# RWKV-7 scan of a hybrid diffusion step: a second pair of array quadrants for the products inside a chunk

## The chip, the cores and the metric

The kernel runs on one core of a Trainium2 chip. A core has five engines with an instruction stream each: TensorE (PE; its weight loads are shown apart as PEld), VectorE (DVE), ScalarE (ACT), GpSimd (POOL) and SyncE (SP), which only issues DMAs here. They wait for each other by semaphores. The metric is the device time of one launch in microseconds; the kernel before has a median of 6051.32 us over three runs, 6049.71 to 6054.07.

## What is computed

One inference step of a backbone with two layers. Each layer has attention beside a bidirectional RWKV-7 time mixing, an output projection, and a retrieval over 16384 experts. The change is in the RWKV part. There 8 heads of width 64 carry a 64x64 state through 640 tokens (128 of context and 512 of a latent grid), once in each direction, and the two results are added:

```python
def _rwkv_step(S, inp):
    r, w, kk, a, k, v = inp
    sk = jnp.einsum('bdhvk,bdhk->bdhv', S, kk)
    S = S * w[..., None, :] - sk[..., :, None] * (kk * a)[..., None, :] + v[..., :, None] * k[..., None, :]
    return S, jnp.einsum('bdhvk,bdhk->bdhv', S, r)
...
    xs = (to_scan(shared(r)), to_scan(per_dir(w)), to_scan(shared(kk)),
          to_scan(per_dir(a)), to_scan(per_dir(kmod)), to_scan(shared(v)))
    s_final, y = lax.scan(_rwkv_step, s0.astype(jnp.float32), xs)
    y = jnp.moveaxis(y, 0, 1)
    y = y[:, :, 0] + jnp.flip(y[:, :, 1], axis=1)
```

## The kernel before

`rwkv_scan` does not step through tokens. It goes through 5 tiles of 128 tokens (`TILES`), each of two chunks of 64 (`CHUNK`), for two streams, one for each direction, that run side by side. `rwkv_scan` is called once a layer, so a launch has 10 tiles for each stream. Nothing in it is a loop on the device: the five tiles are written out, and so is every product. (The two layers are a device loop around it.)

Inside a chunk the token-to-token dependence is a triangular system of 64x64 for each head. The kernel inverts it by doubling: `M` is the inverse for blocks of some size, `MT` its transpose, and a *level* makes them one size larger, from `LT` (the strictly triangular matrix) masked to that level: X = (masked L) x M, then M -= MT' x X and MT -= X' x MT. `LEVELS` is 6, and the loop runs lv = 1 to 5; the last has no update of M.

All in fp32. A product is 64x64x64 for one head `j` (8) and one chunk `c` (2), so 16 products for one stream, 32 for both. The array is four quadrants of 64x64: a product takes the rows (partitions) where its operands lie and the columns (partitions) where its result goes. `quads` is the order (0,0), (1,1), (0,1), (1,0) of row half and column half; `pair_product` and `to_channels` use all four. `chunk_product` reads and writes `rows(c)`: it uses the two quadrants on the diagonal. A fp32 product stands in the trace as two matmul records and two weight-load records, a 128x128 transpose as one and one.

The order of the work is written out by hand: each engine has its own list for a tile, in the same order in every tile, and waits on counting semaphores (`x_done`, `x_taken`, `m_ready`, ...).

- TensorE (`block.tensor`): two pair products a stream for L and P (bank 0, 1), two more for M's start and F (banks 2, 3); `to_tokens`, transposes of a, b and k (L1217); k x r (`GT`); q1 (L1258), the first correction; the levels (L1202); za and zq, the inverse applied to a's tokens and to q1; `to_channels` products (L1211); then the state steps (L1312, L1320).
- ScalarE: copies from PSUM to SBUF: `tokens` (L985: a_tok, nb, kt), `take_q1` (L991), `take_x` (L996), `take_zq`, `take_a`; and `decays` (L980), the exponentials of the next tile, after levels 2 and 3.
- VectorE: `masked` (L1080), M + identity (L1114), MT made from LT (L1117) + identity (L1120), `update` (L1089 for M, L1093 for MT), `ab` of the next tile (L1072 to L1076) after levels 3 and 4, the copy of za (L1132), and the sums of outputs and states (L1135 to L1180).
- GpSimd: `level_mask` (L1038), the masked L of each level, two levels ahead of use, and `rk` (L1050), k and r of the next tile.

`st.ps` is a stream's half of PSUM: four banks of 512 columns. `w.ident2` is a 64x64 identity, once in each half of the rows.

Of the kernel before, what the change touches and what calls it, by code (L numbers as in the profile page):

```python
# [20 lines left out]
ALU = mybir.AluOpType  # L21
# [3 lines left out]
P = 128  # L25
# [915 lines left out]
def rwkv_scan(nc, s, w, layer):  # L941
# [4 lines left out]
             "q1_taken", "pt_ready", "x_done", "x_taken", "mx_done", "mtx_done", "m_ready", "mt_ready", "za_done",  # L946
# [4 lines left out]
    with stage(nc, *["r%d_%s" % (d, n) for d in range(2) for n in names]) as (block, *sems):  # L951
# [20 lines left out]
        def _(act):  # L972
# [10 lines left out]
            def tokens(st, i, n, dst, bank, sign):  # L983
                act.wait_ge(st.e["tr_done"], 3 * i + n)
                nc.scalar.activation(dst.rearrange("p (h b) k -> p h b k", h=2),  # L985
                                     st.ps[:, bank, :].rearrange("p (b h k) -> p h b k", h=2, k=CHUNK), ACT.Copy,
                                     scale=sign).then_inc(st.e["tr_taken"], 1)

            def take_q1(st, i):
                act.wait_ge(st.e["q1_done"], i + 1)  # L990
                nc.scalar.activation(st.q1, st.ps[:, 1, :].rearrange("p (j v) -> p j v", v=CHUNK),  # L991
                                     ACT.Copy).then_inc(st.e["q1_taken"], 1)

            def take_x(st, i, lv):
                act.wait_ge(st.e["x_done"], 5 * i + lv)
                nc.scalar.activation(st.X, st.ps[:, 0, :].rearrange("p (j v) -> p j v", v=CHUNK),  # L996
                                     ACT.Copy).then_inc(st.e["x_taken"], 1)

            def take_zq(st, i):
                act.wait_ge(st.e["zq_done"], i + 1)  # L1000
                nc.scalar.activation(st.zq, st.ps[:, 2, :].rearrange("p (j v) -> p j v", v=CHUNK),
                                     ACT.Copy).then_inc(st.e["zq_taken"], 1)

            def take_a(st, i):
                act.wait_ge(st.e["a_done"], i + 1)
                for c in range(2):
                    nc.scalar.activation(st.A[:, c].rearrange("p b k -> p (b k)"), st.ps[:, 3 * c, 0:256],
# [4 lines left out]
            for i in range(TILES):  # L1012
                for n, bank, sign in ((1, 0, 1.0), (2, 1, -1.0), (3, 0, 1.0)):
                    for st in streams:
                        tokens(st, i, n, (st.a_tok, st.nb, st.kt)[n - 1], bank, sign)
                for st in streams:
                    take_q1(st, i)
                for lv in range(1, LEVELS):
# [46 lines left out]
        def _(dve):  # L1065
# [18 lines left out]
            def update(st, i, lv):  # L1084
                e = st.e
                if lv < LEVELS - 1:
                    dve.wait_ge(e["mx_done"], 4 * i + lv)
                    dve.wait_ge(e["m_ready"], 5 * i + lv)
                    v.tensor_tensor(st.M, st.M, st.ps[:, 2, :].rearrange("p (j t) -> p j t", t=CHUNK),  # L1089
                                    ALU.subtract).then_inc(e["m_ready"], 1)  # L1090
                dve.wait_ge(e["mtx_done"], 5 * i + lv)
# [11 lines left out]
            for i in range(TILES):  # L1103
# [11 lines left out]
                marks = []  # L1115
                for st, link in zip(streams, links):
                    marks.append(link.mark(v.tensor_tensor(st.MT, st.LT, st.mask(4), ALU.mult)))  # L1117
                for st, at in zip(streams, marks):
                    dve.wait_ge(st.e["chain"], at)
                    v.tensor_tensor(st.MT, st.MT, st.ident, ALU.add).then_inc(st.e["mt_ready"], 1)  # L1120
                for st in streams:
                    masked(st, i, 3, st.GT, 2, 0, 2)
                for lv in range(1, LEVELS):
                    for st in streams:
                        update(st, i, lv)
                    if lv == 3 and i + 1 < TILES:
                        ab(streams[0], i + 1)
                    if lv == 4 and i + 1 < TILES:
                        ab(streams[1], i + 1)
                for st in streams:  # L1130
                    dve.wait_ge(st.e["za_done"], i + 1)
                    v.tensor_copy(st.za, st.ps[:, 1, :].rearrange("p (j t) -> p j t", t=CHUNK)).then_inc(st.e["za_taken"], 1)  # L1132
                for st in streams:
                    dve.wait_ge(st.e["r_done"], i + 1)
                    v.tensor_tensor(st.rr.rearrange("p b (c t) -> p c b t", c=2),  # L1135
                                    st.ps[:, 1:3, 0:256].rearrange("p c (b t) -> p c b t", b=RB),
                                    st.rT.rearrange("p b (c t) -> p c b t", c=2), ALU.add).then_inc(st.e["r_taken"], 1)
                for st in streams:
# [6 lines left out]
                    v.tensor_tensor(y_of(st, i), st.ps[:, 1:3, 0:256].rearrange("p c (b t) -> p c b t", b=RB),  # L1145
                                    y_of(st, i), ALU.add).then_inc(st.e["y0_taken"], 1)
                for n in range(2):
                    marks = []
                    for st, link in zip(streams, links):
# [9 lines left out]
                        marks.append(link.mark(v.tensor_tensor(st.sum, st.ps[:, 3 * c, 0:256], now, ALU.add)))  # L1159
# [1381 lines left out]
```

## Time and profile before

| | us |
|---|---|
| median of three runs | 6051.32 |
| lowest, highest | 6049.71, 6054.07 |
| the profiled execution, its own time | 6041.68 |
| its span in the trace | 6039.9 |
| first scan, from 519 to 813 | 294 |
| second scan, from 3484 to 3778 | 294 |

| engine, of the whole span | busy us | share |
|---|---|---|
| TensorE, matmul | 5538.2 | 92% |
| TensorE, weight load | 5352.4 | 89% |
| VectorE | 3316.2 | 55% |
| ScalarE | 2205.1 | 37% |
| GpSimd | 2219.7 | 37% |

The experts take most of the span. The two scans are 588 us of 6039.9. A matmul record's length in the trace (218 ns) is that of one product's way through the array, several of them overlap; how fast products follow each other is read from starts, not from lengths. "issue" behind the idle time of an engine means that it waited for nothing that the profile shows. "PEclk" is the granted clock of TensorE as a share of 2.4 GHz.

### The profile page before, as it was taken

To read this page: it belongs to the slowest core of one execution; us is meant where nothing else is said; L and a number is where in the kernel's file an instruction comes from. 1 tells how busy PE (TensorE), PEld (TensorE's weight loads), DVE (VectorE), ACT (ScalarE), POOL (GpSimd) and SP (SyncE) were. 2 spreads that over 40 slices of the span, in tenths; PEclk is the share of its full clock that TensorE was granted. 3 is DMA by queue.
4 is the path that set the end of the run, shared out by engine and by line. 5 is a ranking of instruction groups with operands and counts; after the bars stand their busy time and mean duration, and the time that the engine had idled before them with its cause. 6 is when DMAs were issued, how large, how long until landed. Compare 5 with 4: busy or idle time off the path is not lost. (4 is left out here: it accounts for less than half of the span.)

```text
span 6039.9 us, 130192 instructions
## 1 busy us (share of the span) xinstructions
PE 5538.2 (92%) x53444; PEld 5352.4 (89%) x53444; DVE 3316.2 (55%) x6178; ACT 2205.1 (37%) x2717; POOL 2219.7 (37%) x1048
## 2 busy tenths in 40 slices
PE   5877897899999999999979688799999999999999
PEld 2757887899999999999968488699999999999999
DVE  4545547756565146566645465496555541656655
ACT  4433222355555622222224332224555564222221
POOL 0002222365566543343300032225556564334332
PEclk8988998999999999999989799899999999999999
DMA  5200012245555565445411000224555556554553
GB/s 200 81 34 13 5 59 84 96 164 177 175 176 182 165 220 174 163 165 175 142 71 51 19 7 17 84 69 135 177 174 180 176 168 226 167 170 163 170 167 111
DMA packets 304063, 778.41 MB, mean 129 GB/s; under 512 B 23724, under 2 KB 109228, under 8 KB 299496
## 3 DMA queue, kind: packets, MB, share of 16 engines
q1 hardware_dynamic: 303592, 771.81, 37.9%
q8 instruction: 335, 5.49, 0.4%
q14 instruction: 136, 1.11, 0.1%
HBM read 586.38 MB, written 185.34 MB: 128 GB/s over the span
## 5 line engine op out<-in xcount | busy, mean ns | idle before, releaser
L2135 POOL TENSOR_TENSOR ex_v_lo<-ex_v_raw,ex_v_hi 128x1024 fp32r<-128x1024 f32 x256 | 692.1, 2724 | 1071.4 <-ACT ex_v_hi L2041 1071.4
L335 PE MATMUL ex_ps<-tk_h_hi,tk_u_hi 128*128 128x320 f32 x4096 | 966.4, 317 | 44.0 <-POOL tk_u_lo L2123 34.8
L2123 POOL TENSOR_TENSOR tk_u_lo<-tk_u_raw,tk_u_hi 128x1024 fp32r<-128x1024 f32 x256 | 655.5, 2561 | 883.2 <-ACT tk_u_hi L2011 870.5
L335 PE MATMUL ex_ps<-ex_wa_hi,ex_v_hi 128*128 128x320 f32 x4096 | 935.1, 310 | 18.8 <-issue 18.8
L335 PE MATMUL ex_ps<-tk_h_hi,tk_u_lo 128*128 128x320 f32 x4096 | 938.3, 310 | 3.8 <-issue 3.8
L335 PE MATMUL ex_ps<-tk_h_lo,tk_u_hi 128*128 128x320 f32 x4096 | 937.0, 310 | 0.0
L335 PE MATMUL ex_ps<-ex_wa_hi,ex_v_lo 128*128 128x320 f32 x4096 | 934.8, 309 | 0.0
L335 PE MATMUL ex_ps<-ex_wa_lo,ex_v_hi 128*128 128x320 f32 x4096 | 934.7, 309 | 0.0
L2295 DVE TENSOR_TENSOR ex_y<-ex_y,ex_ps 128x640 f32<-128x640 f32 x496 | 405.9, 818 | 671.4 <-PE ex_ps L335 666.7
L335 PEld LDWEIGHTS ex_ps<-tk_h_hi,tk_u_hi 128*128 128x128 f32 x4096 | 680.0, 190 | 46.1 <-POOL tk_u_lo L2123 35.7
L335 PEld LDWEIGHTS ex_ps<-ex_wa_hi,ex_v_hi 128*128 128x128 f32 x4096 | 686.5, 188 | 19.3 <-issue 19.3
L335 PEld LDWEIGHTS ex_ps<-tk_h_hi,tk_u_lo 128*128 128x128 f32 x4096 | 688.0, 189 | 4.8 <-issue 4.8
L335 PEld LDWEIGHTS ex_ps<-tk_h_lo,tk_u_hi 128*128 128x128 f32 x4096 | 689.5, 189 | 0.0
L335 PEld LDWEIGHTS ex_ps<-ex_wa_lo,ex_v_hi 128*128 128x128 f32 x4096 | 686.2, 188 | 0.0
L335 PEld LDWEIGHTS ex_ps<-ex_wa_hi,ex_v_lo 128*128 128x128 f32 x4096 | 686.1, 188 | 0.0
L2254 DVE CUSTOM_DVE_ANT_0 ex_ps<-x,tk_silu 128x512 f32<-128x512 f32 x384 | 346.2, 901 | 611.9 <-DMA x<-in_w_mod_rows 599.8
L2130 POOL TENSOR_TENSOR x<-tk_one_hot,tk_g_hk 128x512 f32<-128x512 bf16 x320 | 556.6, 1745 | 82.0 <-PE ex_ps L1944 77.8
L2035 ACT ACTIVATE tk_grid<-ex_ps 128x512 f32<-128x512 f32 x320 | 356.3, 1113 | 474.3 <-PE ex_ps L1944 474.3
L2041 ACT ACTIVATE ex_v_hi<-ex_v_raw 128x1024 fp32r<-128x1024 f32 x256 | 268.3, 1048 | 693.9 <-PE ex_ps L335 693.9
L2046 ACT ACTIVATE ex_wa_hi<-x 128x640 fp32r<-128x640 f32 x256 | 189.4, 740 | 619.9 <-DVE x L2280 619.9
L2028 ACT ACTIVATE x<-tk_one_hot 128x512 f32<-128x512 bf16 x320 | 391.3, 1223 | 17.0 <-issue 9.1
L2286 DVE TENSOR_TENSOR ex_wa_lo<-x,ex_wa_hi 128x640 fp32r<-128x640 f32 x256 | 374.1, 1461 | 30.4 <-ACT ex_wa_hi L2046 21.3
(341 smaller groups left out, 8333.9 us busy)
## 6 DMA issues: line engine op xcount, KB each, us to landing
tk_u_raw<-in_expert_u SPq DMA_DIRECT2D x256, 512.0 KB, 4.2
ex_v_raw<-in_expert_v SPq DMA_DIRECT2D x256, 512.0 KB, 3.6
act_spill<-tk_act_e SPq DMA_DIRECT2D x256, 320.0 KB, 2.3
grid_scratch<-tk_grid SPq DMA_DIRECT2D x160, 512.0 KB, 5.4
ex_g<-grid_scratch SPq DMA_DIRECT2D x64, 1280.0 KB, 11.0
x<-in_w_mod_rows SPq DMA_DIRECT2D x192, 256.0 KB, 4.6
ex_a<-act_spill SPq DMA_DIRECT2D x32, 1280.0 KB, 7.8
x<-act_spill SPq DMA_DIRECT2D x32, 1280.0 KB, 8.0
```

Of the source, the lines that this page charges most:

```text
L335: ins = nc.tensor.matmul(out[:, q, 0:HALF], a, b[:, q * HALF:(q + 1) * HALF], start=(first and n == 0), stop=(last and n == 2))
L2028: nc.scalar.activation(on_j[:, n % S], tokens_of(n // B % 2, 1, n % B), ACT.Copy).then_inc(e["onj"], 1)
L2035: nc.scalar.activation(grid[:, half, :, at * B:(at + 1) * B].rearrange("p i t -> p t i"), ps_g[:, n % S], ACT.Copy).then_inc(e["taken"], 1)
L2041: nc.scalar.activation(v_hi[h][:, k], v_raw[:, k], ACT.Copy).then_inc(e["v_hi"], 1)
L2046: nc.scalar.activation(wa_hi[h][:, k], wa[:, k % 2], ACT.Copy).then_inc(e["wa_hi"], 1)
L2123: nc.gpsimd.tensor_tensor(u_lo[:, at % 2], u_raw[:, at % 3], u_hi[:, at % 2].bitcast(F32), ALU.subtract).then_inc(e["u_split"], 1)
L2130: nc.gpsimd.tensor_tensor(on_i[:, n % S], tokens_of(n // B % 2, 0, n % B), bcast(g_hk[:, at], 2, P), ALU.mult).then_inc(e["oni"], 1)
L2135: nc.gpsimd.tensor_tensor(v_lo[h][:, k], v_raw[:, k], v_hi[h][:, k].bitcast(F32), ALU.subtract).then_inc(e["v_split"], 1)
L2254: last = v.tensor_tensor_reduce(ps_m, w_mod[:, n % 2], silu[:, k, n % 2 * 512:n % 2 * 512 + 512], 1.0, 0.0, ALU.mult, ALU.add, tile_sums[: ...
L2286: v.tensor_tensor(wa_lo[h][:, k], wa[:, k % 2], wa_hi[h][:, k].bitcast(F32), ALU.subtract).then_inc(e["wa_split"], 1)
L2295: v.tensor_tensor(yb, yb, new, ALU.add).then_inc(e["y_added"], 1)
```

## The change

Heads 4 to 7 keep X, MT, a_tok and q1 in the rows of the *other* chunk (`turned`). A product that reads `rows(c)` and writes `turned`, or the other way round, then uses the two off-diagonal quadrants for heads 4 to 7, and `heads()` orders the products so that four follow each other on four quadrants. The update of MT reads both operands and writes its result in the same turned rows. Results of one stream now lie in two banks, a half each (`place`), and the copies and updates read two half banks.

- a's tokens: products of aT with `ident2` instead of transposes, straight into turned rows.
- MT is no longer made on VectorE from LT. TensorE multiplies M by `ident2` into turned rows (`m_turned`), and ScalarE copies it to MT (`take_turned`).
- k x r moves from ahead of the levels to level 1, the transposes of b to level 2, of k to level 3; ScalarE's copies of them follow in levels 2 and 3, `decays` moves to after levels 3 and 4.
- VectorE does both streams' M updates, then both streams' MT updates; `ab` of stream 0 stands after level 4, of stream 1 after level 5.

```diff
+            def take_turned(st, i):
+                act.wait_ge(st.e["m_turned"], i + 1)
+                nc.scalar.activation(pairs(st.MT), two_banks(st, 2, 0), ACT.Copy).then_inc(st.e["mt_ready"], 1)
...
-                    if lv in (2, 3) and i + 1 < TILES:
-                        decays(streams[lv - 2], i + 1)
+                    if lv == 2:
+                        for st in streams:
+                            tokens(st, i, 2, st.nb, -1.0)
+                    if lv == 3:
+                        for st in streams:
+                            tokens(st, i, 3, st.kt, 1.0)
+                    if lv in (3, 4) and i + 1 < TILES:
+                        decays(streams[lv - 3], i + 1)
...
-                marks = []
-                for st, link in zip(streams, links):
-                    marks.append(link.mark(v.tensor_tensor(st.MT, st.LT, st.mask(4), ALU.mult)))
-                for st, at in zip(streams, marks):
-                    dve.wait_ge(st.e["chain"], at)
-                    v.tensor_tensor(st.MT, st.MT, st.ident, ALU.add).then_inc(st.e["mt_ready"], 1)
...
                     for st in streams:
                         update(st, i, lv)
-                    if lv == 3 and i + 1 < TILES:
+                    for st in streams:
+                        update_turned(st, i, lv)
+                    if lv == 4 and i + 1 < TILES:
                         ab(streams[0], i + 1)
-                    if lv == 4 and i + 1 < TILES:
-                        ab(streams[1], i + 1)
+                if i + 1 < TILES:
+                    ab(streams[1], i + 1)
...
-            def chunk_product(st, bank, left, right):
-
-                for j in range(HEADS):
-                    for c in range(2):
-                        last = mm(st.ps[rows(c), bank, rows(j)], left[rows(c), j, :], right[rows(c), j, :], start=True,
-                                  stop=True)
+            def turned(j, c):
+
+                return rows(c if j < RB else 1 - c)
...
+            def heads():
+
+                return [(j, c) for b in range(RB) for j in (b, b + RB) for c in range(2)]
...
+            def chunk_product(st, bank, half, left, right, at, to):
+
+                for j, c in heads():
+                    last = mm(place(st, bank, half, j)[to(j, c), :], left[at(j, c), j, :], right[at(j, c), j, :], start=True,
+                              stop=True)
                 return last
...
-                    to_tokens(st, 0, st.aT)
-                    to_tokens(st, 1, st.bT)
+                    for b in range(RB):
+                        for h, c in quads:
+                            last = mm(place(st, 0, 0, h * RB + b)[turned(h * RB, c), :], st.aT[rows(h), b, rows(c)],
+                                      w.ident2[rows(h), :], start=True, stop=True)
+                    last.then_inc(st.e["tr_done"], 1)
...
+                    pe.wait_ge(st.e["m_ready"], 5 * i + 1)
+                    for j, c in heads():
+                        last = mm(place(st, 2, 0, j)[turned(j, c), :], st.M[rows(c), j, :], w.ident2[rows(c), :],
+                                      start=True, stop=True)
+                    last.then_inc(st.e["m_turned"], 1)
...
+                        chunk_product(st, 0, 0, (st.PT0, st.PT1)[lv % 2], st.M, straight, turned).then_inc(e["x_done"], 1)
...
+                            chunk_product(st, 0, 1, st.MT, st.X, turned, straight).then_inc(e["mx_done"], 1)
...
-                        chunk_product(st, 3, st.X, st.MT).then_inc(e["mtx_done"], 1)
+                        for j, c in heads():
+                            r = turned(j, c)
+                            last = mm(st.ps[r, 3, rows(j)], st.X[r, j, :], st.MT[r, j, :], start=True, stop=True)
+                        last.then_inc(e["mtx_done"], 1)
```

On TensorE, in a tile, between the pair products and the end of level 1, there stood before (a row is a run of equal program instructions, one for each product or transpose; x32 is both streams):

```order
L1217 MATMUL rw_ps<-ident,rw_aT 128x128 x4
L1217 MATMUL rw_ps<-ident,rw_bT 128x128 x4
L1217 MATMUL rw_ps<-ident,rw_aT 128x128 x4
L1217 MATMUL rw_ps<-ident,rw_bT 128x128 x4
L1194 MATMUL rw_ps<-rw_rT,rw_kT 64x64 x32
L1217 MATMUL rw_ps<-ident,rw_kT 128x128 x8
L1258 MATMUL rw_ps<-z,rw_PT 64x64 x32
L1202 MATMUL rw_ps<-rw_M,rw_PT 64x64 x32
L1202 MATMUL rw_ps<-rw_X,rw_MT 64x64 x16
L1202 MATMUL rw_ps<-rw_MT,rw_X 64x64 x16
L1202 MATMUL rw_ps<-rw_X,rw_MT 64x64 x16
L1202 MATMUL rw_ps<-rw_MT,rw_X 64x64 x16
```

At the same place on TensorE now, up to the transposes of b in level 2:

```order
L1281 MATMUL rw_ps<-rw_ident,rw_aT 64x64 x32
L1288 MATMUL rw_ps<-z,rw_PT 64x64 x32
L1294 MATMUL rw_ps<-rw_ident,rw_M 64x64 x32
L1236 MATMUL rw_ps<-rw_M,rw_PT 64x64 x32
L1214 MATMUL rw_ps<-rw_rT,rw_kT 64x64 x32
L1236 MATMUL rw_ps<-rw_X,rw_MT 64x64 x32
L1328 MATMUL rw_ps<-rw_MT,rw_X 64x64 x32
L1236 MATMUL rw_ps<-rw_M,rw_PT 64x64 x32
L1251 MATMUL rw_ps<-ident,rw_bT 128x128 x8
```

a's eight transposes became 32 products, 32 products that turn M are new, and k x r and b's transposes moved into the levels; a level itself has 96 products before and now. The row "M,PT" is X, "X,MT" the update of M, "MT,X" that of MT.

On VectorE, at the end of the levels of a tile, there stood before, from stream 0's last update of M in level 4 to the copy of za:

```order
L1089 TENSOR_TENSOR rw_M<-rw_M,rw_ps 128x512
L1093 TENSOR_TENSOR rw_MT<-rw_MT,rw_ps 128x512
L1072 TENSOR_TENSOR rw_aT<-rw_W,mix 128x512
L1075 COPY rw_WC<-rw_W 128x8
L1076 TENSOR_TENSOR rw_bT<-rw_W,z 128x512
L1093 TENSOR_TENSOR rw_MT<-rw_MT,rw_ps 128x512 x2
L1132 COPY rw_PT<-rw_ps 128x512 x2
```

And now on VectorE, from the updates of level 4 on:

```order
L1116 TENSOR_TENSOR rw_MT<-rw_MT,rw_ps 128x512 x2
L1091 TENSOR_TENSOR rw_aT<-rw_W,mix 128x512
L1094 COPY rw_WC<-rw_W 128x8
L1095 TENSOR_TENSOR rw_bT<-rw_W,z 128x512
L1116 TENSOR_TENSOR rw_MT<-rw_MT,rw_ps 128x512 x2
L1091 TENSOR_TENSOR rw_aT<-rw_W,mix 128x512
L1094 COPY rw_WC<-rw_W 128x8
L1095 TENSOR_TENSOR rw_bT<-rw_W,z 128x512
L1151 COPY rw_PT<-rw_ps 128x512 x2
```

The second `ab` moved from ahead of the last MT updates to between them and the copy of za.

## Rows read from the trace of the kernel before

**Rows 1.** Page, part 1: busy us, share of the span, instructions of each engine.
```profile
PE 5538.2 (92%) x53444; PEld 5352.4 (89%) x53444; DVE 3316.2 (55%) x6178; ACT 2205.1 (37%) x2717; POOL 2219.7 (37%) x1048
```

**Rows 2.** Stretches, the two scans: us; busy PE, PEld, DVE, ACT, POOL; PEclk; DMA; GB/s.
```profile
519.00:813.00 294.00, 259.69 (x9720) 252.05 (x9720) 174.67 (x301) 79.67 (x150) 88.96 (x70) 0.97 0.02 6
3484.00:3778.00 294.00, 260.66 (x9505) 249.95 (x9500) 172.16 (x296) 83.39 (x154) 86.51 (x67) 0.99 0.05 15
```

**Rows 3.** DMA queues, 519 to 813, then 740 to 761: packets, MB, share of 16 engines.
```profile
q8 instruction: 76, 1.25, 1.7%
...
q8 instruction: 5, 0.08, 1.7%
```

**Rows 4.** Timeline, levels 2 and 3 of tile 0: start us, us, engine, line, operands, count.
```profile
543.56 1.95 PEld L1202 LDWEIGHTS rw_ps<-rw_M,rw_PT 64*64 64x64 f32 x64
...
549.16 1.95 PEld L1202 LDWEIGHTS rw_ps<-rw_M,rw_PT 64*64 64x64 f32 x64
...
550.37 0.60 ACT L996 ACTIVATE rw_X<-rw_ps 128x512 f32<-128x512 f32 x1 [2.51 <-PE rw_ps L1202]
...
551.03 1.02 PEld L1202 LDWEIGHTS rw_ps<-rw_X,rw_MT 64*64 64x64 f32 x32
```

**Rows 5.** Timeline of PEld, end of tile 0 and start of tile 1; in brackets idle before.
```profile
568.99 0.37 PEld L1211 LDWEIGHTS rw_ps<-rk,rw_PT 64*64 64x64 f32 x19 [0.31 <-issue]
...
572.99 0.14 PEld L1211 LDWEIGHTS rw_ps<-rw_PT,rk 64*64 64x64 f32 x3 [2.05 <-issue]
...
588.71 0.44 PEld L1194 LDWEIGHTS rw_ps<-rw_rT,rw_bT 64*64 64x64 f32 x24 [2.14 <-issue]
589.06 0.56 PEld L1194 LDWEIGHTS rw_ps<-rw_bT,rw_aT 64*64 64x64 f32 x32
589.52 0.56 PEld L1194 LDWEIGHTS rw_ps<-rw_rT,rw_bT 64*64 64x64 f32 x32
590.15 0.42 PEld L1217 LDWEIGHTS rw_ps<-ident,rw_aT 128*128 128x128 f32 x4
```

**Rows 6.** Timeline of PEld, end of tile 3 and start of tile 4.
```profile
740.85 0.15 PEld L1211 LDWEIGHTS rw_ps<-rk,rw_PT 64*64 64x64 f32 x4 [0.45 <-issue]
...
744.87 0.15 PEld L1211 LDWEIGHTS rw_ps<-rw_PT,rk 64*64 64x64 f32 x4 [2.06 <-issue]
...
760.05 0.25 PEld L1194 LDWEIGHTS rw_ps<-rw_rT,rw_bT 64*64 64x64 f32 x9 [1.85 <-issue]
```

**Rows 7.** Groups of instructions, 519 to 813: busy us, mean ns; idle before.
```profile
L1038 POOL TENSOR_TENSOR rw_PT<-rw_LT,rw_masks 128x512 f32<-128x512 f32 x50 | 63.0, 1282 | 109.9 <-DVE rw_LT L1080 48.0 <-PE rw_ps L1258 34.5 <-PE rw_ps L1202 27.4
...
L1093 DVE TENSOR_TENSOR rw_MT<-rw_MT,rw_ps 128x512 f32<-128x512 f32 x50 | 34.4, 687 | 16.5 <-PE rw_ps L1202 16.5
...
L996 ACT ACTIVATE rw_X<-rw_ps 128x512 f32<-128x512 f32 x50 | 29.9, 597 | 79.0 <-PE rw_ps L1202 79.0
```

**Rows 8.** Timeline of DVE, level 4 of tile 1.
```profile
619.30 0.68 DVE L1072 TENSOR_TENSOR rw_aT<-rw_W,mix 128x512 f32<-128x512 f32 x1
...
619.98 0.68 DVE L1076 TENSOR_TENSOR rw_bT<-rw_W,z 128x512 f32<-128x512 f32 x1
```

**Rows 9.** Timeline of PEld, end of tile 1.
```profile
629.22 0.13 PEld L1211 LDWEIGHTS rw_ps<-z 64*64 64x64 f32 x2 [1.19 <-issue]
...
632.67 0.13 PEld L1211 LDWEIGHTS rw_ps<-rk,z 64*64 64x64 f32 x2 [1.50 <-issue]
```

**Rows 10.** Stretches around stops of TensorE; columns as in rows 2.
```profile
569.90:573.30 3.40, 1.49 (x103) 1.35 (x96) 1.29 (x2) 0.36 (x2) 2.39 (x2) 1.00 0.03 5
573.30:576.70 3.40, 3.14 (x124) 2.95 (x114) 0.00 (x0) 0.00 (x0) 0.10 (x1) 0.51 0.02 5
...
740.00:761.00 21.00, 14.35 (x736) 13.28 (x728) 11.06 (x23) 1.53 (x5) 4.98 (x4) 1.00 0.02 4
```

**Rows 11.** Timeline of PEld, first products of tile 0, at half the clock.
```profile
528.19 0.99 PEld L1194 LDWEIGHTS rw_ps<-rw_bT,rw_aT 64*64 64x64 f32 x32
529.05 0.99 PEld L1194 LDWEIGHTS rw_ps<-rw_rT,rw_bT 64*64 64x64 f32 x32
```

More of the change, by code:

```diff
@@ L1012, in _ @@
             for i in range(TILES):
-                for n, bank, sign in ((1, 0, 1.0), (2, 1, -1.0), (3, 0, 1.0)):
-                    for st in streams:
-                        tokens(st, i, n, (st.a_tok, st.nb, st.kt)[n - 1], bank, sign)
+                for st in streams:
+                    take_a_tok(st, i)
                 for st in streams:
                     take_q1(st, i)
+                for st in streams:
+                    take_turned(st, i)
                 for lv in range(1, LEVELS):
@@ L1158, in _ @@
                             dve.wait_ge(e["chain"], 1)
-                        marks.append(link.mark(v.tensor_tensor(st.sum, st.ps[:, 3 * c, 0:256], now, ALU.add)))
+                        marks.append(link.mark(v.tensor_tensor(st.sum, st.ps[:, c, 0:256], now, ALU.add)))
                     for at, st, link in zip(marks, streams, links):
@@ L1164, in _ @@
                             dve.wait_ge(st.e["out_done"], 16)
[L1165 removed]
+                        v.tensor_tensor(st.state[1 - n], st.ps[:, 2, 0:256], st.sum, ALU.add).then_inc(st.e["chain"], 1)
                         link.n += 1
@@ L1244, in _ @@
                     pe.wait_ge(st.e["prod_taken"], 5 * i + 2)
[L1245 to L1246 removed]
+                    for b in range(RB):
[3 more added lines that the diff above has]
+                    last.then_inc(st.e["tr_done"], 1)
+                for st in streams:
+                    pe.wait_ge(st.e["tr_taken"], 3 * i + 1)
+                    val = value(st, i)
+                    for j, c in heads():
+                        last = mm(place(st, 0, 0, j)[turned(j, c), :], st.PT0[rows(c), j, :], val(c, j), start=True, stop=True)
+                    last.then_inc(st.e["q1_done"], 1)
                 for st in streams:
                     pe.wait_ge(st.e["prod_taken"], 5 * i + 4)
[L1249 to L1259 removed]
+                    pe.wait_ge(st.e["m_ready"], 5 * i + 1)
[3 more added lines that the diff above has]
+                    last.then_inc(st.e["m_turned"], 1)
                 for lv in range(1, LEVELS):
@@ L1311, in _ @@
                             for h in range(2):
-                                last = mm(st.ps[rows(h), 1, rows(b)], st.A[rows(h), c, b, :], now[rows(h), rows(b)],
+                                last = mm(st.ps[rows(h), 2, rows(b)], st.A[rows(h), c, b, :], now[rows(h), rows(b)],
                                           start=True, stop=True)
```

97 lines of the change are left out of this document (55 added, 42 removed).

## The prediction

> **What bounds the kernel now.** I read the page first: TensorE is busy for 92% of the span, but the change touches only the two scans [rows 1]. The second view is busy time by stretch, for the two scans: 294 us each, TensorE busy for 260 of them, VectorE 173, ScalarE and GpSimd under 90, DMA share 2 to 5% [rows 2]. So within the scan it is TensorE's stream that sets the pace, and the question is what sets the pace of that stream.
>
> The third view, the DMA queues over the same stretches, answers it. A queue of kind "instruction" moves 76 packets with 1.25 MB in the first scan [rows 3]. TensorE has 9720 + 9720 = 19440 records there [rows 2]. 1.25 MB over 19440 is 64 bytes for each, and 19440 / 76 is 256 instructions for a packet of 16 KB. The scan is written out, without a loop, so its program comes in once, packet by packet, and one packet comes about every 3.8 us (294 / 76 is 3.87 with the scan's start and end, where TensorE stands idle). In the 21 us from 740 to 761 there are 5 [rows 3].
>
> Two kinds of stretch show what that means. In the levels every product of 64x64 uses the two diagonal quadrants. Sixteen products are 32 matmul records; 64 records take 1.87 us (549.16 to 551.03), 29.2 ns each, without a gap [rows 4]. 256 instructions are 128 of these and 128 weight loads: 3.74 us of array work, just what a packet takes. In the products that already use four quadrants 32 records take 0.46 us (589.06 to 589.52), 14.4 ns each [rows 5], so 256 instructions are worked off in 1.9 us. There TensorE stops: the weight loads resume six times between 568.99 and 588.71 (three of them shown), each time after idle time that is put down to "issue", nothing that another engine or a semaphore released [rows 5]. The mean of the five distances is 19.72 / 5 = 3.94 us. In tile 3 it is the same from 740.85 to 760.05: 19.20 / 5 = 3.84 [rows 6]. Nearly a packet each, however few products lie in it. My reading: **the instructions of TensorE arrive at 256 per 3.4 to 4.1 us, and the scan already runs at that rate throughout**; what is saved in the array turns into waiting for the next packet.
>
> A cross-check by the period of a tile: the same product resumes at 572.99 in tile 0 and at 744.87 in tile 3 [rows 5, 6], 57.3 us a tile. A tile has 19440 / 5 = 3888 instructions, 15.2 packets, so 3.77 us each, the levels included.
>
> **The change, part by part.** (1) *Products on four quadrants.* Per tile and both streams, X (160 products), M's update (128), q1 (32), za and zq (64) go from two quadrants to four: 384 products, 768 records, at 29.2 - 14.4 = 14.8 ns, 11.4 us of array time. The products that update MT (L1328) stay on the diagonal, since both operands of heads 4 to 7 now lie in the same other rows. Number of instructions: unchanged. By the reading above this is worth nothing, because a level (two streams, 96 products of four instructions: 384, 1.5 packets) still needs 1.5 x 3.77 = 5.66 us to arrive, and now takes 5.6 (543.56 to 549.16) [rows 4].
>
> (2) *Would the other engines let it go faster?* Now stream 0's copy of X starts at 550.37, 1.21 us after X (549.16), of which 0.93 are the product and 0.28 are between; it takes 0.60, and M's product starts 0.06 later, at 551.03 [rows 4]. After: X of both streams 2 x 0.46; stream 0's copy is through at 0.46 + 0.28 + 0.60, M's product starts at 1.40 (0.48 idle), stream 1's at 1.96 (0.10 idle) and ends at 2.42; MT 1.87 more: 4.3 us. The copies are 597 ns on ScalarE, and 4 x 0.6 on VectorE, 2 x 1.28 on GpSimd in a level [rows 7]. All below 5.66, so none of them is late, and the idle 0.58 lies inside packet waits.
>
> (3) *a's tokens* by products with ident2 in place of 8 full transposes: 8 x 2 = 16 instructions go, 32 products x 4 = 128 come (the order shows x32 in place of two x4). (4) *TensorE turns M*: 32 products more, 128 instructions, and two ScalarE copies of 0.60; VectorE loses four passes of the size of its updates, 0.69 [rows 7], which stood beside TensorE's work. Sum of (3) and (4): **+240 instructions a tile**. In array time that is little: 64 records of 14.4 ns are 0.92 us for M, and a's 0.92 replace about as much in transposes (eight, four of which take 0.42) [rows 5]. In arrivals it is 240 / 256 = 0.94 packet, x 3.77 = 3.5 us a tile, x 10 tiles = **+35 us**.
>
> (5) *More waits.* 50 more instructions a scan carry waits, and where several are due an instruction of its own may stand. Between 0 and 50 more a scan is 0 to 0.2 packet, 0 to 1.5 us for both scans; I take 1.
>
> (6) *VectorE's a and b of the next tile, stream 1,* now stand between the last update and the copy of za: from 619.30 to 620.66, 1.4 us with the small copy between them [rows 8], in 4 tiles of 5. Queued behind it is za's copy, and TensorE waits for that. The cover: za and zq are 256 instructions, one packet, 3.8 us, of which the array needs 1.9; the copy of stream 0 ends 0.9 + 1.4 + 0.7 = 3.0 us after the last MT product. Costed at 0; without the cover it would be 8 x 1.4 = 11 us.
>
> (7) *kT x rT and the transposes of b and k* move from ahead of the levels into levels 1 to 3: the same instructions, another place. 0.
>
> **The sum.** Against the profiled execution's own 6041.68 us (span 6039.9): + 35 + 1 = 6078. That execution lies 9.6 us below the median of the runs, 6051.32; the difference carried over gives **6087 us**, 0.6% slower.
>
> **Bounds of the cost of a packet.** Waiting for packets throughout, a tile would have (3888 + 240) / 256 = 16.1 of them. At the slower measured mean, 3.94, 63.5 us a tile against 57.3: +62 over ten tiles, 6113. At the quickest distance shown, 3.45 (629.22 to 632.67) [rows 9], 55.6: -17, 6034. I take 3.77, since it is a mean over 46 packets in which both kinds of stretch occur.
>
> **Rivals.** *A, the array is the bound and the change pays.* Then (1) counts: -11.4, +0.9 for M and five waits of 0.58 that nothing fills, +2.9: -7.6 a tile, -76 us, **5975**. For it: 29.2 ns is also what the array itself seems to need, and in the levels no gap is seen [rows 4]. Against it: the stops of 2 us in the stretches with four quadrants [rows 5, 6], for which the profile knows no releaser. It decides if packets can come in clearly under 3.4 us when asked for sooner; no row shows one. The Trainium skill speaks for this rival: "Runtime: NRT & Kernel Launch", section "Instruction fetch mechanics", holds that instructions come in blocks of 256 and that fetching is hidden since dispatch is slower than the fill. The block size agrees with 256 per packet here; the hiding does not agree with the stops of up to 2.14 us. By that rule the sum would be rival A's.
>
> *B, packets come quicker when each is waited for.* Mean 3.45 gives 6034, 3.6 gives 16.1 x 3.6 = 58.1, +8 us, 6059. For it: distances of 3.45 occur; against: five in a row at 3.94.
>
> *C, TensorE's clock falls, and the diagonal products become the bound.* The row from 573.3 to 576.7 has a granted clock of 0.51, half of 2.4 GHz, and what stands before it is 1.9 us of idle TensorE (busy 1.49 of 3.40) [rows 10]. After the change such idle time stands in every packet that is all four-quadrant, some eight a tile. At half clock 32 four-quadrant records take 0.86 us (528.19 to 529.05) [rows 11], so a level would be 64 + 64 such records, 3.4, and 64 diagonal ones at 58 ns, 3.7, with 0.6 of waiting: 7.7 against 5.66 us. If a third of the 50 levels ran so: +34 on top of +36, **6121**; the point from which it costs is a level beyond 5.66. Against it: from 740 to 761, with stops of 2.06 and 1.85 us among five [rows 6], the clock stayed at 1.00 [rows 10].
>
> *D, the moved work fills the stops and so takes back what is added.* It would need 36 us of stops to vanish, and the stops shown sit at the end of a tile, where no instruction goes or comes; I give it nothing.
>
> **Numbers.** Forecast (all between 6070 and 6105) 0.66; C 0.14; B 0.12 (0.02 below 6039, 0.08 to 6063, 0.02 above); A 0.08. A measurement of this kernel can tell about 0.2%, 12 us, from no change. Faster by more: 0.08 + 0.02 = 0.10. Within: 0.08. Slower: 0.66 + 0.14 + 0.02 = 0.82. The range takes in B's middle and C up to its third: 6050 to 6120.
>
> **What would show it.** In the changed profile: 80 or 81 instruction packets in the first scan and about 312 us for it; TensorE's weight loads stopping for "issue" inside the levels, at distances of 3.4 to 4.1 us; a level still at 5.6 to 5.7 us; busy TensorE down to some two thirds. Wrong if a level takes 4.3 us, or if packets stand under 3.4 us apart; wrong in size if half clock shows for long in the scans.

## The result

The changed kernel takes 6081.06 us (median of 5 runs, 6079.87 to 6088.17); the kernel before took 6051.32 beside it (6048.65 to 6055.32). The ratio is 1.0048, 95% interval 1.0035 to 1.0060: 0.5% slower, as forecast (6087, range 6050 to 6120). In a second comparison, after_again below, the same kernel gave 1.0037 (1.0023 to 1.0052). Its profiled execution took 6079.87 us, 38.2 more than that of before (6041.68).

The page, part 1 (busy us, share, instructions) and the instruction queue of part 3, changed kernel:
```profile
PE 5470.1 (90%) x54644; PEld 5267.4 (87%) x54644; DVE 3309.4 (54%) x6138; ACT 2211.2 (36%) x2737; POOL 2226.6 (37%) x1048
...
q8 instruction: 345, 5.65, 0.4%
```
TensorE has 1200 matmuls and 1200 weight loads more than in [rows 1], and is busy 68 us less. Before, the same queue had this:
```profile
q8 instruction: 335, 5.49, 0.4%
```
Ten packets more. Then the two scans by stretch (columns as in [rows 2]), and the packets of the first:
```profile
519.00:833.00 314.00, 225.54 (x10320) 209.31 (x10320) 162.35 (x280) 82.27 (x160) 90.20 (x70) 0.97 0.02 6
3505.00:3817.00 312.00, 227.58 (x10231) 209.98 (x10224) 160.02 (x277) 83.61 (x161) 86.56 (x68) 0.98 0.03 9
...
q8 instruction: 81, 1.33, 1.8%
```
Against [rows 2, 3] the first scan is 20 us longer, while TensorE is busy 34 us less in it: 72% of the stretch where it was 88%. 76 packets became 81. The idle time is in the waits of the weight loads (line, releaser: us in total, times, longest). First the kernel before, 519 to 813:
```profile
PEld rw_ps L1211 <- issue: 16.3, 13, 2.1
...
PEld rw_ps L1194 <- issue: 9.5, 12, 2.1
```
and the changed kernel, 519 to 835:
```profile
PEld rw_ps L1236 <- issue: 29.6, 39, 1.8
PEld rw_ps L1245 <- issue: 25.2, 15, 2.1
PEld rw_ps L1214 <- issue: 11.9, 8, 1.9
...
PEld rw_ps L1328 <- issue: 8.2, 10, 1.8
```
L1236 and L1328 are the products of the levels, L1236 those of za and zq too (L1202 before, which has no such row at all). TensorE's weight loads now stop 49 times there, and no engine and no semaphore ends the stops; the rows of the matmuls themselves say the same ("issue", 23.9 us in 28 stops of L1236 and 6.9 in 10 of L1328). The timeline of levels 2 to 4 of tile 1 shows where (start us, us, operands, count; in brackets idle before and its end):
```profile
606.92 0.78 PEld L1328 LDWEIGHTS rw_ps<-rw_MT,rw_X 64*64 64x64 f32 x24 [1.35 <-issue]
607.57 1.07 PEld L1236 LDWEIGHTS rw_ps<-rw_M,rw_PT 64*64 64x64 f32 x64
...
610.92 0.68 PEld L1236 LDWEIGHTS rw_ps<-rw_X,rw_MT 64*64 64x64 f32 x33 [0.65 <-issue]
...
614.60 0.68 PEld L1236 LDWEIGHTS rw_ps<-rw_M,rw_PT 64*64 64x64 f32 x35 [0.68 <-issue]
...
616.38 1.02 PEld L1236 LDWEIGHTS rw_ps<-rw_X,rw_MT 64*64 64x64 f32 x64 [0.17 <-issue]
617.30 0.66 PEld L1328 LDWEIGHTS rw_ps<-rw_MT,rw_X 64*64 64x64 f32 x19
618.34 1.42 PEld L1328 LDWEIGHTS rw_ps<-rw_MT,rw_X 64*64 64x64 f32 x45 [0.38 <-issue]
...
622.04 0.73 PEld L1236 LDWEIGHTS rw_ps<-rw_X,rw_MT 64*64 64x64 f32 x44 [0.60 <-issue]
...
625.98 0.83 PEld L1236 LDWEIGHTS rw_ps<-rw_M,rw_PT 64*64 64x64 f32 x49 [1.06 <-issue]
```
64 records on four quadrants take 0.92 us (616.38 to 617.30), on two they took 1.87 [rows 4]. But the resumptions at 606.92, 610.92, 614.60, 618.34, 622.04 and 625.98 stand 4.00, 3.68, 3.74, 3.70 and 3.94 us apart, 3.81 in the mean, in the middle of products that have all their operands. What the array saved is spent waiting for instructions.

The trace also holds the start of every instruction packet, and that ties the stops to the packets. The last packets to start before these six resumptions did so at 604.27, 608.24, 612.30, 615.74, 619.51 and 623.80, 2.2 to 2.7 us ahead of them. Over both scans of the changed kernel, 135 of the 137 "issue" stops of more than 0.5 us end 2.1 to 3.0 us after a packet's start; in the kernel before all 41 do. Nor is it a fixed price of each instruction: between the stops the records on four quadrants follow each other at 14.4 ns.

### The profile page after: what moved, and what is told of

It is laid out like the page before. It is cut to its first block and busy times, and to the rows that moved or that the text cites. A ratio compares the mean times of both kernels' runs of the same rounds, so it can differ in the third digit from the quotient of the medians.

```text
span 6078.1 us, 132652 instructions
## 1 busy us (share of the span) xinstructions
PE 5470.1 (90%) x54644; PEld 5267.4 (87%) x54644; DVE 3309.4 (54%) x6138; ACT 2211.2 (36%) x2737; POOL 2226.6 (37%) x1048
## 3 DMA queue, kind: packets, MB, share of 16 engines
q1 hardware_dynamic: 303592, 771.81, 37.7%
q8 instruction: 345, 5.65, 0.4%
## 5 line engine op out<-in xcount | busy, mean ns | idle before, releaser
L2182 POOL TENSOR_TENSOR x<-tk_one_hot,tk_g_hk 128x512 f32<-128x512 bf16 x320 | 569.9, 1786 | 71.8 <-PE ex_ps L1996 66.7
L2080 ACT ACTIVATE x<-tk_one_hot 128x512 f32<-128x512 bf16 x320 | 391.8, 1225 | 20.1 <-issue 12.2
```

The source lines that it names most:

```text
L2080: nc.scalar.activation(on_j[:, n % S], tokens_of(n // B % 2, 1, n % B), ACT.Copy).then_inc(e["onj"], 1)
L2182: nc.gpsimd.tensor_tensor(on_i[:, n % S], tokens_of(n // B % 2, 0, n % B), bcast(g_hk[:, at], 2, P), ALU.mult).then_inc(e["oni"], 1)
```

## The experiments

The table is worked out from each kernel's trace: both scans' length from their first to their last record, packets per scan, the mean distance from the first packet to the last, and TensorE's instructions in a tile. The kernel before has one trace, from the first comparison. "Own" is the profiled execution's time. The ratio is to the kernel before, timed on the same chip.

| kernel | instructions a tile | packets | distance, scan 1 / 2 | scans, us | own, us | ratio (95%) |
|---|---|---|---|---|---|---|
| before | 3888 | 76 + 76 | 3.75 / 3.77 | 588.4 | 6041.68 | 1 |
| changed | 4128 | 81 + 81 | 3.78 / 3.77 | 625.9 | 6079.87 | 1.0048 (1.0035-1.0060) |
| after_again | 4128 | 81 + 81 | 3.74 / 3.73 | 619.2 | 6064.57 | 1.0037 (1.0023-1.0052) |
| p1_before_240 | 4128 | 81 + 81 | 3.80 / 3.76 | 621.5 | 6069.62 | 1.0040 (1.0026-1.0055) |
| p2_before_480 | 4368 | 86 + 86 | 3.85 / 3.77 | 665.0 | 6116.94 | 1.0121 (1.0104-1.0138) |
| p3_before_half | 3888 | 76 + 76 | 3.76 / 3.72 | 585.5 | 6045.20 | 1.0003 (0.9993-1.0013) |
| p4_after_half | 4128 | 81 + 81 | 3.85 / 3.76 | 630.1 | 6079.67 | 1.0060 (1.0043-1.0076) |
| p5_after_ab | 4128 | 81 + 81 | 3.76 / 3.72 | 622.2 | 6069.39 | 1.0040 (1.0025-1.0054) |
| p5_again | 4128 | 81 + 81 | 3.72 / 3.75 | 619.9 | 6072.35 | 1.0042 (1.0028-1.0056) |
| p6_before_wide | 3888 | 76 + 76 | 3.82 / 3.84 | 598.9 | 6049.36 | 1.0018 (1.0009-1.0028) |
| p7_after_fewer | 3896 | 77 + 76 | 3.83 / 3.84 | 603.9 | 6058.00 | 1.0024 (1.0015-1.0034) |
| x1_transpose | 3568 | 70 + 70 | 3.90 / 3.93 | 564.1 | 6018.09 | 0.9955 (0.9941-0.9969) |
| x2_merge | 3312 | 65 + 65 | 3.92 / 3.92 | 526.3 | 5990.03 | 0.9909 (0.9892-0.9925) |
| x3_merge_ab | 3312 | 65 + 65 | 3.93 / 3.90 | 525.3 | 5984.90 | 0.9906 (0.9892-0.9920) |

**Instructions alone.** The kernel before, with 6 small products more in each of its ten pair products a tile, 240 instructions. They repeat products in place, for 4 of 64 columns; the second kernel does 12.
```diff
 def pair_product(st, bank, half, left, right):
     ...
+    for n in range(6):
+        b, (h, c) = n // 4, quads[n % 4]
+        at = 256 * half + CHUNK * b
+        last = mm(st.ps[rows(c), bank + h, at:at + 4], left[rows(h), b, rows(c)],
+                  right[rows(h), b, CHUNK * c:CHUNK * c + 4], start=True, stop=True)
```


> The kernel before, and in each pair product (four quadrants, at the start of a tile, where TensorE already stands idle for 'issue') six of its products are repeated for 4 columns only: 60 products, 240 TensorE instructions a tile, with hardly any array work. Theory (instructions of TensorE arrive at one packet of 256 per 3.77 us): +0.94 packet a tile, +35 us, 6086. Rival (array time counts, and the stops have another cause): 120 records of at most 14.4 ns are 1.7 us a tile, beside stops of 1 to 2 us: 0 to +17 us, 6051 to 6068. By the theory the first scan has 80 or 81 instruction packets.

> The same with twelve repeated products of 4 columns in each pair product: 480 more TensorE instructions a tile. Theory: twice the cost of the dose before, +70 us, 6121, and 85 packets in the first scan. Rival: 240 records of at most 14.4 ns, 0 to +35 us, and no proportion to the number of instructions.

Measured: 6067.97 beside 6043.4, +24.6 us, and 6117.16, +73.8. The scans in the two traces are 33.1 and 76.6 longer than before's. The first scan of each, the stretch and then its packets:
```profile
519.00:834.00 315.00, 275.28 (x10320) 267.95 (x10320) 174.91 (x301) 79.66 (x150) 88.54 (x70) 0.96 0.02 6
...
q8 instruction: 81, 1.33, 1.8%
```
```profile
519.00:859.00 340.00, 294.74 (x10920) 286.89 (x10920) 175.40 (x301) 79.53 (x150) 88.46 (x70) 0.91 0.03 7
...
q8 instruction: 86, 1.41, 1.7%
```
The single dose beside the changed kernel is the strongest evidence here. With the old quadrants, layout and order, and TensorE busy for 275 us, the scan takes 315 us; the changed kernel, with the same 10320 matmuls and 81 packets, is busy for 226 us and takes 314. Fifty us of array time make no difference; the number of instructions does. In medians the single dose falls short of its 35 us, the double dose does not (70 expected). In the scans themselves they are near 35 and 70, as above. The rest of the launch, which none of these edits touches, takes 5444 to 5462 us from trace to trace, and totals carry that spread.

**Array time alone.** The level products write and read 32 columns in place of 64, in the kernel before and in the changed one, with as many instructions. VectorE's updates of M and MT are halved with them.
```diff
-def chunk_product(st, bank, left, right):
+def chunk_product(st, bank, left, right, cols=CHUNK):
 ...
-    last = mm(st.ps[rows(c), bank, rows(j)], left[rows(c), j, :], right[rows(c), j, :], start=True,
-              stop=True)
+    last = mm(st.ps[rows(c), bank, CHUNK * j:CHUNK * j + cols], left[rows(c), j, :],
+              right[rows(c), j, 0:cols], start=True, stop=True)
```


> The kernel before with the level products for 32 of 64 columns: the same number of instructions, half the array work in the levels. (The numbers of the inverse are given up for it: X is copied with a factor of 0, and M and MT are updated in half of their columns, so VectorE's updates are shorter too.) Theory: the levels still need a packet per 256 instructions, a level stays at 5.6 us, total 6030 to 6055. Rival (the array bounds the levels): a level falls from 5.6 towards 4 us, five levels in ten tiles, -50 to -80 us, 5970 to 6000.

> The changed kernel with the level products for 32 of 64 columns, the same kind of cut (X copied with a factor of 0, updates of half the columns). Theory: nothing moves against the changed kernel, 6070 to 6090, the same packets. Rival (part of the levels is bound by the chain of array, ScalarE and VectorE): 20 to 60 us less than the changed kernel.

Measured: 1.0003 and 1.0060 (6077.87 us). The first is no evidence, because the edit didn't take array time away. PEld in two products of a level, p3_before_half:
```profile
561.28 1.95 PEld L1202 LDWEIGHTS rw_ps<-rw_M,rw_PT 64*64 64x64 f32 x64
563.15 1.95 PEld L1202 LDWEIGHTS rw_ps<-rw_MT,rw_X 64*64 64x64 f32 x64
```
64 records with half the columns still take 1.87 us, 29.2 ns each, as in [rows 4]. (The weight loads are 64x64 as before; the edit halves only what streams against them.) The second kernel tells something else: from their first packet to their last its scans lie at half clock (1.2 GHz) for 135 us, against 16 in the changed kernel. Two such stretches (columns as in [rows 2]):
```profile
625.20:635.40 10.20, 10.20 (x287) 10.20 (x287) 5.04 (x12) 1.79 (x3) 0.00 (x0) 0.50 0.01 3
666.10:683.20 17.10, 16.41 (x377) 15.82 (x370) 3.86 (x9) 3.68 (x7) 4.40 (x4) 0.50 0.01 3
```
There TensorE is busy nearly throughout and slower than the supply: 17.10 us for 377 matmuls is 45 ns each, where a packet brings 128 in 3.77 us, 29 ns. The packets follow: of the distances between them, the 33 that lie mostly at half clock are 4.10 us in the mean, the other 127 are 3.73. So by this count 135 us of half clock cost 33 x 0.37 = 12 us, and the scans are only 4.2 us longer than the changed kernel's.

**Fewer instructions.** Two kernels that keep the changed kernel's layout in chunk and quadrant but turn M by full 128 x 128 transposes, 4 for each stream (16 instructions against 128 for both in the change), at the start and in levels 1 to 4, where they also replace the products that update MT. VectorE then copies MT. The second also puts a's tokens and q1 side by side, likewise nb and FT, so that one product of 128 columns does what two of 64 did.
```diff
+def turn(st):
+    for b in range(RB):
+        last = tr(st.ps[:, 3, b * P:(b + 1) * P],
+                  st.M[:, 2 * b:2 * b + 2, :].rearrange("p h t -> p (h t)"), s.ident[:])
 ...
+    if lv < LEVELS - 1:
+        v.tensor_copy(st.MT, new).then_inc(e["mt_ready"], 1)
+    else:
+        v.tensor_tensor(st.MT, st.MT, new, ALU.subtract).then_inc(e["mt_ready"], 1)
 ...
+h["aq"] = wb("aq%d" % d, 2 * D_R)[:]
+h["a_tok"], h["q1"] = h["aq"][:, 0:D_R], h["aq"][:, D_R:2 * D_R]
```


> The changed kernel with another way to MT: X, MT, a_tok and q1 lie in the rows of the head's half, and MT is made in each of levels 1 to 4 (and at the start) by four full transposes of M (8 instructions a stream) in place of sixteen products (64). The result is the same. 3568 TensorE instructions a tile, against 3888 before and 4128 in the changed kernel. Theory (3.77 us for a packet of 256): -1.25 packets a tile against before, -47 us, 6004, and 70 or 71 packets in the first scan. Rival (array time and the chain of copies): M's update now stands ahead of MT on the chain, so a level has a wait more (VectorE 0.69, transposes, copy 0.69): a level of 5 us or more and no gain on before.

> x1_transpose, and products that share their weights are made as one with 128 columns: MT with [a_tok | q1], za with [nb | F]. The array streams as many columns, the products are 32 + 32 fewer: 3312 TensorE instructions a tile. ScalarE and VectorE wait for each other at two banks. Theory: -2.25 packets a tile against before, -85 us, 5966, 65 or 66 packets in the first scan. Rival (the chain of copies takes over where packets no longer bound): the same time as x1_transpose.

Measured: 6018.09 and 5992.52 beside 6047.93, -30 and -55 us. The sign and the packets (70 and 65) are as expected, the size is two thirds. x2_merge, its first scan and packets, then PEld inside a level:
```profile
520.00:788.00 268.00, 212.44 (x8280) 190.03 (x8281) 159.54 (x281) 82.80 (x161) 89.35 (x70) 0.96 0.03 8
...
q8 instruction: 65, 1.06, 1.7%
```
```profile
603.51 1.02 PEld L1255 LDWEIGHTS rw_ps<-rw_M,rw_PT 64*64 64x64 f32 x64 [0.17 <-issue]
604.61 0.86 PEld L1282 LDWEIGHTS rw_ps<-ident,rw_kT 128*128 128x128 f32 x8
605.63 1.02 PEld L1261 LDWEIGHTS rw_ps<-rw_X,rw_MT 64*64 64x64 f32 x64 [0.17 <-issue]
607.20 0.42 PEld L1267 LDWEIGHTS rw_ps<-ident,rw_M 128*128 128x128 f32 x4 [0.54 <-issue]
607.79 0.42 PEld L1267 LDWEIGHTS rw_ps<-ident,rw_M 128*128 128x128 f32 x4 [0.18 <-issue]
```
Here the waits are short and stand at the borders of the steps (M's product, M's update on VectorE, turn), not at every 256th instruction: the chain of a level has become the limit in places. That shows in the packets too: 3.92 us apart, one in ten over 4.75. Of x2_merge's 79 "issue" stops of more than 0.5 us, 28 don't end 2.1 to 3.0 us after a packet's start, where 2 of 137 didn't in the changed kernel. From level 4 to 5 these kernels take 4.5 us. Where fewer instructions are asked for, the chain sets the end for part of the time and the price of a packet isn't gained in full. How much of the missing third is the chain's was not separated.

**The place of VectorE's a and b.** In the changed kernel, stream 1's moves from behind the last update to level 4:
```diff
         if lv == 4 and i + 1 < TILES:
             ab(streams[0], i + 1)
-    if i + 1 < TILES:
-        ab(streams[1], i + 1)
+            ab(streams[1], i + 1)
```


> The changed kernel with VectorE's a and b of stream 1 back after level 4 instead of behind level 5. Theory (waits of that size lie under the arrival of packets): no difference to the changed kernel, within 5 us. Rival (VectorE's 1.4 us ahead of za's copy are on the path in 8 tiles): 11 us less than the changed kernel.

> The changed kernel once more, beside p5_again, x3 and p7 on the same chip, so that differences of 5 to 10 us can be read. It should stand 30 to 38 us over the kernel before.

> p5_after_ab once more, beside the changed kernel on the same chip (it stood 10 us under it, on another one). Theory (the 1.4 us lie under the arrival of packets): within 5 us of after_again. Rival (they are on the path): 11 us less than after_again.

> x2_merge with VectorE's a and b of stream 1 back after level 4. In x2_merge packets stand 3.92 us apart in the mean instead of 3.77, so part of a tile waits for the chain of copies and not for packets. If the 1.4 us ahead of za's copy are part of that, this is 5 to 11 us faster than x2_merge, 5982 to 5988; if they are still covered, it is the same.

Measured: 1.0040 in one comparison; in the other, on one chip, 6072.35 us with the move and 6067.76 without, intervals that overlap almost wholly. In x3_merge_ab, the same edit in x2_merge, 0.9906 against 0.9909. The place costs nothing that can be measured, as was costed. x3_merge_ab, 5988.91 us, is level with x2_merge; both beat the kernel before and the changed one. after_again itself stands 20.1 us over the kernel before, where 30 to 38 were expected: a miss that comes up again below.

**Array time added.** In the kernel before, three of four pair products write 128 columns in place of 64, with as many instructions.
```diff
-last = mm(st.ps[rows(c), bank + h, 256 * half + CHUNK * b:256 * half + CHUNK * b + CHUNK],
-          left[rows(h), b, rows(c)], right[rows(h), b, rows(c)], start=True, stop=True)
+n, at = P if b < RB - 1 else CHUNK, 256 * half + CHUNK * b
+flat = right.rearrange("p b t -> p (b t)")
+last = mm(st.ps[rows(c), bank + h, at:at + n], left[rows(h), b, rows(c)],
+          flat[rows(h), P * b + CHUNK * c:P * b + CHUNK * c + n], start=True, stop=True)
```


> The kernel before, and three of four products in each pair product have 128 moving columns instead of 64 (the surplus is overwritten by the next product): the same number of instructions and more array work, about 24 x 10 records a tile at 27 instead of 14.4 ns, 3 us a tile. Theory: the stretch waits for packets anyway, 0 to +5 us. Rival (array work sets the time): +30 us.

Measured: 6057.98, +10 us. The same place as [rows 5], PEld at the start of tile 1:
```profile
584.12 0.90 PEld L1196 LDWEIGHTS rw_ps<-rw_aT,rw_kT 64*64 64x64 f32 x32
584.89 0.90 PEld L1196 LDWEIGHTS rw_ps<-rw_aT,rw_bT 64*64 64x64 f32 x32
...
587.85 0.64 PEld L1196 LDWEIGHTS rw_ps<-rw_rT,rw_bT 64*64 64x64 f32 x24 [0.40 <-issue]
```
32 records take 0.77 us where they took 0.46, and the stop of 2.14 us is 0.40 here. There are 320 pair records a tile, so 320 x 9.7 ns = 3.1 us more array time, 31 in ten tiles; two thirds of it were hidden in the stops, 10 us were not. The cover is real but not quite as deep as the stops suggest, and 10 us are more than the 0 to 5 expected, if far from the rival's 30. The 76 packets are as many as before and stand 3.83 us apart instead of 3.76: when a packet comes isn't wholly independent of what TensorE does with the one before.

**The changed order without its instructions.** The changed kernel with a's tokens from 2 products of 16 a stream, and M turned by 1 of 16 (3896 instructions a tile, before has 3888). MT's copy is scaled to 0.
```diff
-        for b in range(RB):
-            for h, c in quads:
+        for b in range(1):
+            for h, c in quads[0:2]:
 ...
-        for j, c in heads():
+        for j, c in heads()[0:1]:
             last = mm(place(st, 2, 0, j)[turned(j, c), :], st.M[rows(c), j, :], w.ident2[rows(c), :],
```


> The changed kernel with its four-quadrant levels, but without most of the products that it adds: 2 of 16 products for a's tokens and 1 of 16 for turning M in each stream (MT is copied with a factor of 0, so the numbers are given up): 3896 TensorE instructions a tile, as before (3888). Theory: with the same number of instructions four quadrants are worth nothing: the time of the kernel before, 0 to 5 us over it, 76 packets in the first scan. Rival (array time counts): the levels' saving shows, 10.5 us a tile less array work, 30 to 80 us under the kernel before.

Measured: 6062.24, +14.5 us, its scans 15.5 us longer than before's. Rival A (-30 to -80) is out: with four quadrants and no more instructions than before, nothing is gained. But 14.5 us are also more than 0 to 5. PEld at the head of a tile of the second scan, p7_after_fewer:
```profile
3615.66 1.05 PEld L1288 LDWEIGHTS rw_ps<-z,rw_PT 64*64 64x64 f32 x64 [0.71 <-ACT rw_a_tok L992]
3618.40 0.19 PEld L1294 LDWEIGHTS rw_ps<-rw_ident,rw_M 64*64 64x64 f32 x2 [1.69 <-issue]
3620.07 0.19 PEld L1294 LDWEIGHTS rw_ps<-rw_ident,rw_M 64*64 64x64 f32 x2 [1.48 <-issue]
```
For the weight loads this is "issue". The groups of the first scan, 519 to 830 (busy us, mean ns; idle before), say what the matmuls behind them wait for:
```profile
L1137 DVE TENSOR_TENSOR rw_M<-rw_M,rw_ident 128x512 f32<-128x512 f32 x10 | 12.4, 1282 | 0.0
...
L1294 PE MATMUL rw_ps<-rw_ident,rw_M 64*64 64x64 f32 x20 | 3.8, 284 | 8.0 <-DVE rw_M L1137 8.0
```
M's turn waits for VectorE's addition of the identity (L1137). Here that takes 1.28 us in the mean, against 0.68 in the kernel before, where GpSimd never works at the same time. At the place shown above, VectorE and GpSimd have these rows:
```profile
3616.71 3.24 DVE L1137 TENSOR_TENSOR rw_M<-rw_M,rw_ident 128x512 f32<-128x512 f32 x2
```
```profile
3616.46 2.94 POOL L1057 TENSOR_TENSOR rw_PT<-rw_LT,rw_masks 128x512 f32<-128x512 f32 x2 [2.98 <-PE rw_ps L1288]
...
3621.22 1.27 POOL L1057 TENSOR_TENSOR rw_PT<-rw_LT,rw_masks 128x512 f32<-128x512 f32 x1 [1.81 <-PE rw_ps L1236]
```
The third GpSimd pass, alone, takes 1.27. The same two groups in the changed kernel:
```profile
L1137 DVE TENSOR_TENSOR rw_M<-rw_M,rw_ident 128x512 f32<-128x512 f32 x10 | 8.6, 898 | 0.0
...
L1294 PE MATMUL rw_ps<-rw_ident,rw_M 64*64 64x64 f32 x320 | 6.7, 221 | 3.5 <-issue 2.4 <-DVE rw_M L1137 1.0
```
8.0 us in the first scan there, 1.0 here; in the second 8.6 and 1.1. The time went where these waits are: six distances between packets in p7_after_fewer, each at the head of a tile, are 5.57 to 7.80 us, together 17 us more than six of 3.77. So the 16.6 us of waiting can account for the +14.5, but no run takes the wait away. Some 23 us at half clock lie in the same six distances (53 us in all, from the first packet to the last of each scan, against 13 in the kernel before), and what part is theirs isn't told apart. My reading is that TensorE arrives later in the changed kernel, since a's tokens and the turn are themselves a packet a tile, and finds M ready: a price that stands in place of the instructions, not beside them.

## Why the prediction was right

**The bound.** Confirmed. The scan's pace is that of TensorE's instruction packets: 81 packets (80 or 81 forecast), 314 us for the first scan (312), stops for "issue" inside the levels at 3.7 to 4.0 us (3.4 to 4.1), and from level 4 to 5, where nothing else changed, 5.65 us in the mean of ten (5.6 to 5.7; 5.60 before), measured from one copy of X to the next. Single ones run from 5.13 to 6.11, as a level is one and a half packets. TensorE's busy share came out at 72%, not two thirds. Over both scans 10 packets x 3.77 = 37.7 us, and the scans grew by 37.5. Part (2) reads [rows 7] too low in one place, VectorE's four updates in a level at 0.6 us where the row has 687 ns; nothing hangs on it.

**Four quadrants, worth 0.** Confirmed by p1_before_240 beside the changed kernel; p7_after_fewer shows no gain either, though beside its own wait a gain of a few us could lie hidden. The forecast of a level's chain, 4.3 us, is not shown directly; x2_merge, whose levels 4 to 5 take 4.5 with fewer packets, is the nearest.

**+240 instructions, +35 us.** The term is right in the profiled execution (+38.2 in all, forecast +36). In medians it is smaller: +30 in the first comparison, +20 beside after_again, +24.6 for the dose alone. The distance of packets is no constant. From trace to trace its mean runs from 3.72 to 3.80 us at 81 packets (p4_after_half, with its half clock, aside), and for the changed kernel alone from 3.78 and 3.77 to 3.74 and 3.73: 162 x 0.04 = 6 us.

**Where the 6 us come from, and what was luck.** The forecast of 6087 lies 6 us over the median of 6081.06. The last step of the sum, which carries over the 9.6 us between the profiled execution of before and its median, compares medians with medians and is in order. What was too large, measured so, is the +36: 29.7 us in this comparison, 20.1 in the second. The profiled executions differ by more, 38.2, because that of before (6041.68) lies under all five of the runs timed in the first comparison (from 6048.65), while that of the changed kernel lies 1.2 under its median. That the forecast came within 6 us is thus partly luck: in the second comparison the same difference is little more than half of what was forecast. The sign and the mechanism are not luck, as the doses and the packets show.

**Waits and placing.** The +1 for waits can't be told from 0. The place of a and b: 0, by three kernels. Moved work, 0: from level 1 to level 4 the steps now take 7.83, 6.31 and 6.06 us instead of 5.6, since they hold k x r and the transposes. That and level 4 to 5 make 3.4 us, and the rest of the tile, from which this work went and in which the 240 instructions stand, grew by 0.7: 61.6 against 57.5 us. One mechanism was missed: that M's turn makes VectorE's addition of the identity a step of TensorE's own chain. TensorE waits for it 16.6 us where the 240 instructions are taken away, and 2.1 in the kernel as it is.

**Rivals.** A (5975) is out by p7_after_fewer. The Trainium skill, "Runtime: NRT & Kernel Launch", section "Instruction fetch mechanics", speaks for it by calling a block's cost mostly hidden; its 256 instructions a block agree with every row here (20640 records, 81 packets), the hiding disagrees with the doses. B, packets sooner when asked for: at most a little, 3.73 at full clock in p4_after_half where there was time to make up; never 3.45 in the mean. C, half clock: it occurs, 16 us in the changed kernel's scans, and with 135 us of it p4_after_half's scans are some 4 us longer. The supply leaves slack that a slow stretch uses up. D: no stops vanished.

**Open.** What sets 3.4 to 4.1 us for a packet was not tried; no kernel here changes how instructions are stored or fetched. The traces do show its parts. A packet takes 0.9 to 1.5 us, two never overlap, and in no scan of the 14 traces do two start less than 3.26 us apart. In the changed kernel TensorE resumes 2.54 us after a packet's start (median of the 85 stops over 1 us), and the next packet starts 1.17 us after that (median; never under 1.05). So one packet is fetched at a time. What the 2.5 us after its start consist of, and what starts the next one, stays open. Why the single dose cost 25 us in medians and 33 in its scans can't be told from run-to-run spread.

## What to carry over

In code that is written out, count TensorE's instructions and not only its array time. Read the instruction queue's packets over the stretch and the distance between stops that are put down to "issue"; if the first times some 3.8 us is the stretch, it is fewer instructions that help: here one 128 x 128 transpose or one wide product beat many 64 x 64 ones on more quadrants. When the count falls, look at once for the chain behind it, which takes over before the whole gain is in. Judge a change by medians taken beside each other, and more than once if it is small: one profiled execution can lie 10 us from its median, and the same change cost 30 us in one comparison and 20 in the other.

## What the hardware showed that was not expected

- 64 x 64 products on the diagonal quadrants take 29.2 ns a record with 64 columns and with 32. The Trainium skill, "TensorEngine Tiling (Array Packing)", section "Instruction Overhead", has a fixed cost of about 60 cycles a matmul, an estimate of 25 ns at 2.4 GHz, 4 ns under this flat price. It doesn't fit the 14.4 ns a record on four quadrants [rows 5]. Every matmul record here has a 64x64 weight load beside it in both kernels, so whether the matmul or the weight load sets the 29.2 ns isn't shown.
- On four quadrants 32 records of which 24 have 128 columns take 0.77 us, 24 ns each, and with 64 columns throughout 14.4 ns: from 64 to 128 columns they count.
- A wait of a matmul on another engine appears in the weight loads' row as "issue" (L1294 above). Whether "issue" is a packet or a wait is told by the distance of the stops and by the matmuls' own group.
- Two engines that add to each other's time: VectorE's 128x512 addition of 0.68 us took 1.6 (3.24 for two) while GpSimd's two passes took 2.94 instead of 2.5. In p7_after_fewer 16 of the 20 additions lie more than half under a GpSimd pass and take 1.44 us in the mean, up to 1.76; in the kernel before none does, and all 20 take 0.68 or 0.69.
